# Two layers' front end on one core: layer 1's ada parts put between attention heads, one PSUM bank for probabilities, out product by row halves, router order

## What is computed

```python
hn = rmsnorm(x, g_mix); proj = hn @ w_in        # q, k, v, c_q, c_kv, k_pe, gate_a, gate_b
y_a = moba_attention(q_a, k_a, v_a)             # 8 heads, causal, 64 wide
y_b = causal_attention(q_b, k_b, v_b)           # 8 heads, 96 wide
merged = sigmoid(gate_a) * (y_a @ w_branch_a) + sigmoid(gate_b) * (y_b @ w_branch_b)
x = x + merged @ w_out
x = x + routed_experts(rmsnorm(x, g_ffn), ...)  # top 4 of 32 experts, clamped SwiGLU
hp = rmsnorm(x, g_ple); x = x + sigmoid(hp @ w_ple_gate) * (p @ w_ple_proj)
for l in range(2):
    shift, scale, gate = split(silu(c) @ w_ada[l] + b_ada[l], 3)
    ...
```

## Time and profile before

| what | value |
|---|---|
| median of 3 runs | 1425.66 us |
| the profiled execution | 1425.22 us, span 1423.0 us |
| PE busy | 1337.5 us (94%) |
| PEld, DVE, ACT, POOL busy | 712.5, 479.2, 316.1, 36.2 us |
| moved by DMA | 498.75 MB, mean 351 GB/s |
| chain that ended last | PE 60%, DMA 24%, DVE 6%, ACT 2% |

### The profile page before, as it was taken

The page is one execution under the profiler, slowest core; times in us unless marked ns, Lnnn a source line. Parts: engine busy times, 40 slices in busy tenths (PEclk is TensorE's granted clock), DMA queues, the critical chain, the costliest instruction groups (busy, mean ns, idle before and its releaser), DMA issues.

```text
span 1423.0 us, 16623 instructions
## 1 busy us (share of the span) xinstructions
PE 1337.5 (94%) x6794; PEld 712.5 (50%) x6794; DVE 479.2 (34%) x696; ACT 316.1 (22%) x416; POOL 36.2 (3%) x50
## 2 busy tenths in 40 slices
PE   8989999999999999999899999898999989999998
PEld 5758866334334333333333333333333336897996
DVE  3676665112112111211121111211112116775764
ACT  4254633011111110110111101111011114632531
POOL 2110100000000000000000000000000000000000
PEclk9999999999999999999999999999999999999999
DMA  9982397999999999999999999999999996355330
GB/s 326 387 323 89 107 380 322 418 428 428 428 428 428 428 429 428 429 428 427 429 429 428 428 429 428 427 429 429 428 429 429 428 408 207 120 183 192 125 120 30
DMA packets 76975, 498.75 MB, mean 351 GB/s; under 512 B 7095, under 2 KB 8586, under 8 KB 52362
## 3 DMA queue, kind: packets, MB, share of 16 engines
q1 hardware_dynamic: 75802, 496.06, 85.3%
q0 software_dynamic: 704, 2.10, 0.5%
q10 hardware_dynamic: 432, 0.07, 0.0%
HBM read 497.06 MB, written 1.05 MB: 350 GB/s over the span
## 4 chain that ended last, share of the span: by engine, by line
PE 60%; DMA 24%; DVE 6%; ACT 2%; issue 1%; POOL 0%; SPq 0%; DVEq 0%; ACTq 0%
PE ps L1765 31%; DMA ring<-in_w_gate_up_dram 21%; PE ps L1501 5%; PE ps L1503 5%; PE ps L1502 5%; PE ps L1759 3%; DMA arena<-in_w_gate_up_dram 2%; PE ps L1746 1%; PE ps L1830 1%; ACT arena L760 1%; PE ps L1522 1%; PE ps L1769 1%; PE ps L1523 1%; PE ps L1528 1%; DVE ring_low L891 1%
## 5 line engine op out<-in xcount | busy, mean ns | idle before, releaser
L1765 PE MATMUL ps<-ring,arena 128*64 128x512 f32 x2304 | 518.1, 600 | 33.1 <-DMA ring<-in_w_gate_up_dram 22.1
L1765 PEld LDWEIGHTS ps<-ring,arena 128*64 128x64 f32 x2304 | 159.4, 138 | 364.5 <-issue 300.3
L1765 PE MATMUL ps<-arena 128*64 128x512 f32 x768 | 175.2, 608 | 5.2 <-ACT arena L760 3.3
L1251 DVE TENSOR_SCALAR arena<-ps 128x512 f32<-128x512 f32 x32 | 22.1, 692 | 347.6 <-PE ps L1765 347.6
L753 ACT ACTIVATE arena<-arena 128x512 f32<-128x512 f32 x32 | 20.2, 630 | 498.6 <-DVE arena L1251 498.6
L1765 PEld LDWEIGHTS ps<-arena 128*64 128x64 f32 x768 | 53.7, 139 | 117.3 <-issue 102.2
L1503 PE MATMUL ps<-arena_highs,w_low 128*128 128x256 f32 x384 | 108.4, 282 | 0.0
L1210 DVE TENSOR_SCALAR esel<-const 128x128 fp32r<-128x128 f32 x49 | 12.6, 286 | 278.9 <-ACT arena L764 141.0
L764 ACT COPY arena<-ps 64x512 f32<-64x512 f32 x64 | 37.1, 580 | 239.6 <-PE ps L1765 239.2
L1230 DVE TENSOR_TENSOR X<-X,ps 128x1024 f32<-128x1024 f32 x34 | 41.4, 1218 | 124.2 <-PE ps L1759 124.2
L1501 PE MATMUL ps<-arena_highs,ring_highs 128*128 128x256 f32 x256 | 72.0, 281 | 2.3 <-DVE HT_r L1291 2.3
(11 more groups left out here) (284 smaller groups left out, 1591.9 us busy)
## 6 DMA issues: line engine op xcount, KB each, us to landing
ring<-in_w_gate_up_dram SPq DMA_DIRECT2D x96, 2048.0 KB, 31.2
ring<-in_w_down_dram SPq DMA_DIRECT2D x48, 2048.0 KB, 34.7
arena<-in_w_gate_up_dram SPq DMA_DIRECT2D x32, 2048.0 KB, 32.2
ring<-in_w_in_dram SPq DMA_DIRECT2D x38, 1024.0 KB, 7.2
arena<-in_w_down_dram SPq DMA_DIRECT2D x16, 2048.0 KB, 34.3
ring<-in_w_ada_dram SPq DMA_DIRECT2D x24, 1024.0 KB, 10.2
ring<-in_w_out_dram SPq DMA_DIRECT2D x12, 1024.0 KB, 7.4
ring<-in_w_ple_gate_dram SPq DMA_DIRECT2D x4, 1024.0 KB, 26.9
```

The lines of the kernel that those rows point to most:

```text
L1251: V.tensor_scalar(glu, ps[:, 0, :], LIMIT, None, ALU.min).then_inc(s["g_ready"], 1)
L1765: last = T.matmul(ps[at:at + CAP, bank, :], lhsT, w(g), start=False, stop=stop)
```

## The change

- Layer 1's twelve ada parts, with their chunks in `order1`, go into heads 0, 1, 2, 4, 5, 6, 8, 9, 10, 12, 13 and 14, each behind the head's `project`. They add into bank 3.
- The transposed probabilities of all heads go through bank 1; so a head's transposes wait for the copy of the head before, where they waited for the copy of two before. The pairs of kTb0, kTb1, mod0 and A0 change.
- ScalarE copies layer 1's ada rows out behind the cast of o0's first half, and TensorE waits for that ahead of A1 (`ada_out` 8). The rows go to the part of `const` that held the causal mask, and on to `tabs`. SyncE's `ada_moved(1)` stands behind the load of bin 4, ahead of bins 0 to 3.
- The out product goes over all (h, g) for row half 0, then over row half 1. The first columns of merged stand directly ahead of it, the second between.
- The router of half 1 comes ahead of both `choose`, its columns directly behind `route(0)`. Fillers: one ahead of `route(1)`, four between the counts, where two and three ada parts were.
- `yslot` is cleared by GpSimd, `shares(0)` goes to behind `routed`, and the gathered tokens are moved in two halves.

```diff
-        ada_rows = [view(24, 512), ht_flat[:, 1024:1536]]
-        ada_mods = [view(26, 512, "p (r n) -> p r n", r=4), ht_flat[:, 1536:2048].rearrange("p (r n) -> p r n", r=4)]
+        ada_rows = [view(24, 512), const[:, C_CAUSAL:C_CAUSAL + 512]]
+        ada_mods = [view(26, 512, "p (r n) -> p r n", r=4), tabs[:, 0:512].rearrange("p (r n) -> p r n", r=4)]
...
-        order1 += [(name, kh) for name in ("ga0", "ga1", "gb0", "gb1") for kh in range(2)]
-        order1 += [("A0", 0), ("B0", 0)] + [("ada1", i) for i in range(4)] + [("A1", 0), ("B1", 0)]
-        order1 += [("ada1", i) for i in range(4, 8)] + [(name, kh) for name in ("o0", "o1") for kh in range(2)]
-        order1 += [("ada1", i) for i in range(8, 2 * ADA_COLS)]
+        ada1_at = [h for h in range(2 * HEADS) if h % 4 != 3]
+        for j, (name, kh) in enumerate((name, kh) for name in ("ga0", "ga1", "gb0", "gb1") for kh in range(2)):
+            at_head = [[("ada1", ada1_at.index(h))] if h in ada1_at else [] for h in (2 * j, 2 * j + 1)]
+            order1 += at_head[0] + [(name, kh)] + at_head[1]
+        order1 += [("A0", 0), ("B0", 0), ("A1", 0), ("B1", 0)] + [(name, kh) for kh in range(2) for name in ("o0", "o1")]
...
-                  (("B1", 0), at64[:], None), (("o0", 0), at56[:], ("A0", 0)), (("o0", 1), ring11, ("B0", 0)),
-                  (("o1", 0), ring10, ("A1", 0)), (("o1", 1), at64[:], ("B1", 0))]
+                  (("B1", 0), at64[:], None), (("o0", 0), at56[:], ("A0", 0)), (("o1", 0), ring11, ("B0", 0)),
+                  (("o0", 1), ring10, ("A1", 0)), (("o1", 1), at64[:], ("B1", 0))]
...
-                             ("qTb0", 2, N), ("qTb1", 0, N), ("kTb0", 1, N), ("mod0", 0, N), ("kTb1", 2, N),
+                             ("qTb0", 2, N), ("qTb1", 0, N), ("kTb0", 2, N), ("kTb1", 0, N), ("mod0", 1, N),
                              ("gb0", 2, used1("gb0")), ("gb1", 2, used1("gb1")), ("yTa", 2, N), ("yTb", 0, N),
-                             ("A0", 1, used1("A0")), ("B0", 2, used1("B0")), ("A1", 0, used1("A1")),
+                             ("A0", 3, used1("A0")), ("B0", 2, used1("B0")), ("A1", 0, used1("A1")),
...
-        ADA_BANK = 7
+        ADA_BANK = [7, 3]
+        PROB_BANK = 1
...
-        RT_BANK, POS_BANK = 2 * U1["fT0"][0], 2 * U1["fT0"][0] + 1
+        RT_BANK, POS_BANK = [2 * U1["fT0"][0], 2 * U1["A0"][0]], 2 * U1["fT0"][0] + 1
...
             for k in (4, 0, 1, 2, 3):
                 phase1_left(k)
                 load(0, k)
+                if k == 4:
+                    ada_moved(1)
             sp.wait_ge(s["chunk_used1"], used1("o1"))
             load(0, GROUPS - 1)
             load(1, BINS - 1)
-            ada_moved(1)
...
+            pool.wait_ge(s["chunk_used1"], N1)
+            for a in yslot:
+                G.memset(a, 0.0).then_inc(s["y_cleared"], 1)
...
             w1_high("o0", 0)
+            ada_out(1)
+            w1_high("o1", 0)
             w1_high("o0", 1)
-            w1_high("o1", 0)
             w1_high("o1", 1)
...
+            for h in range(HALVES):
                 act.wait_ge(s["lg_ready"], h + 1)
                 A.activation(ex[:, h, :], lg[:, h, :], ACT.Exp, bias=st[:, 4 + h:5 + h]).then_inc(s["expd"], 1)
-            ada_out(1)
...
-                V.tensor_copy(probT[:, h % 2, :], ps[:, 2 * (h % 2) + 1, 0:3 * P]).then_inc(s["t_free"], 1)
+                V.tensor_copy(probT[:, h % 2, :], ps[:, PROB_BANK, 0:3 * P]).then_inc(s["t_free"], 1)
...
                 if g:
+                    w1_low("o1", 0)
                     w1_low("o0", 1)
-                    w1_low("o1", 0)
...
-            norm_of_x(0)
+            mean_of_x(0)
             columns_of_x(0)
+            power_of_x(0)
             low_part(0)
+            x_sum(1)
+            columns_of_x(1)
+            mean_of_x(1)
             choose(0)
-            shares(0)
-            x_sum(1)
-            norm_of_x(1)
-            columns_of_x(1)
+            power_of_x(1)
             choose(1)
...
-            run(V.memset(yslot[0], 0.0))
-            V.memset(yslot[1], 0.0).then_inc(s["y_ready"], 1)
-            shares(1)
+            for h in range(HALVES):
+                shares(h)
             join()
...
+            dve.wait_ge(s["y_cleared"], 2)
+            dve.sem_inc(s["y_ready"], 1)
             dve.wait_ge(s["routed"], 1)
-            dve.wait_ge(s["gather_done"], 1)
-            gathered()
+            for j, done in enumerate(("gather_half", "gather_done")):
+                dve.wait_ge(s[done], 1)
+                rows = slice(4 * j, 4 * j + 4)
+                ins = V.tensor_tensor(xg[:, rows, :], ps[:, 2 + j, :].rearrange("p (a b) -> p a b", a=4),
+                                      gain8[:, rows].unsqueeze(2).to_broadcast([P, 4, P]), ALU.mult)
+                if j:
+                    ins.then_inc(s["xg_ready"], 1)
+                else:
+                    run(ins)
...
             def transpose_probs(h):
-                bank = 2 * (h % 2) + 1
                 pe.wait_ge(s["prob_done"], h + 1)
-                if h >= 2:
-                    pe.wait_ge(s["t_free"], h - 1)
+                if h >= 1:
+                    pe.wait_ge(s["t_free"], h)
                 for b in range(3):
-                    last = T.transpose(ps[:, bank, b * P:b * P + P], prob[:, h % 2, b * P:b * P + P], ident)
+                    last = T.transpose(ps[:, PROB_BANK, b * P:b * P + P], prob[:, h % 2, b * P:b * P + P], ident)
                 last.then_inc(s["t_full"], 1)
...
+                    if h in ada1_at:
+                        ada_part(1, ada1_at.index(h))
...
-                if g:
-                    columns_of_merged(0)
-                ada_parts(1, 4 * g, 4 * g + 4)
-            columns_of_merged(1)
-
+                    if g + br == 1:
+                        pe.wait_ge(s["ada_out"], 8)
...
-            out_product(0, 0)
-            out_product(0, 1)
-            out_product(1, 0)
+            columns_of_merged(0)
+            for h in range(HALVES):
+                for g in range(2):
+                    out_product(h, g, (0,))
+            columns_of_merged(1)
+            for h, g in ((0, 0), (0, 1), (1, 0)):
+                out_product(h, g, (1,))
             columns_of_x(0)
-            out_product(1, 1, (0,))
+            out_product(1, 1, (1,))
             route(0)
-            out_product(1, 1, (1,))
-            ada_parts(1, 8, 10)
             columns_of_x(1)
+            keep_busy(2, 1)
+            route(1)
             pe.wait_ge(s["mask_done"], 1)
             count(0, before, 0)
             count(E, ones, 0)
             count(2 * E, ones, 0)
-            ada_part(1, 10)
-            route(1)
-            ada_part(1, 11)
-            keep_busy(2, 2)
+            keep_busy(2, 4)
...
+                if k == 3:
+                    last.then_inc(s["gather_half"], 1)
```

More of the change, by code:

```diff
@@ L241, in build @@
         out_stored dve_step pow_in pow_out tables_done
-        x_sums col_highs col_lows w1_highs w1_lows t1_highs mod1_full mod1_moved c_sigmoid cwide_zero cwide_ready q_ready k_ready mlaq_ready mlak_ready
+        x_sums y_cleared gather_half col_highs col_lows w1_highs w1_lows t1_highs mod1_full mod1_moved c_sigmoid cwide_zero cwide_ready q_ready k_ready mlaq_ready mlak_ready
         s_full s_free scored prob_done t_full t_free pv_done y_done
@@ L680, in ada_out @@
                 for r in range(0, P, 32):
-                    A.copy(ada_rows[l][r:r + ADA_COLS, :], ps[r:r + ADA_COLS, ADA_BANK, :]).then_inc(s["ada_out"], 1)
+                    A.copy(ada_rows[l][r:r + ADA_COLS, :], ps[r:r + ADA_COLS, ADA_BANK[l], :]).then_inc(s["ada_out"], 1)
             w1_high("ga1", 0)
@@ L1119, in columns_of_x, with mean_of_x, power_of_x @@
                               ).then_inc(moved1[p], 1)
-            def norm_of_x(h):
+            def mean_of_x(h):
                 dve.wait_ge(s["ffn_sums"], h + 1)
                 V.tensor_scalar(st[:, h:h + 1], st[:, h:h + 1], 1.0 / D, EPS, ALU.mult, ALU.add).then_inc(s["pow_in"], 1)
+            def power_of_x(h):
                 power()
@@ L1133, in choose @@
                 dve.wait_ge(s["rt_full"], h + 1)
-                run(V.scalar_tensor_tensor(lg[:, h, :], ps[:, RT_BANK, h * E:h * E + E], st[:, h:h + 1], b_rt,
+                run(V.scalar_tensor_tensor(lg[:, h, :], ps[:, RT_BANK[h], h * E:h * E + E], st[:, h:h + 1], b_rt,
                                            ALU.mult, ALU.add))
@@ L1537, in ada_part @@
                     at, n = 32 * k, 4 * (i % 2) + k
-                    last = T.matmul(ps[at:at + ADA_COLS, ADA_BANK, :],
+                    last = T.matmul(ps[at:at + ADA_COLS, ADA_BANK[l], :],
                                     cwide[:, n, ADA_COLS - 1 - i // 2:2 * ADA_COLS - 1 - i // 2],
@@ L1714, in route @@
                 for k in range(KC):
-                    last = T.matmul(ps[:, RT_BANK, h * E:h * E + E], HT[:, k, h * P:h * P + P], wr[:, k, :],
```

(1 more changed line is left out.)

1 line of the change is left out of this document (added).

## The result

| what | before | after |
|---|---|---|
| median | 1425.62 us (4 runs) | 1445.30 us (4 runs, 1442.46 to 1446.88) |
| profiled execution, span | 1425.22, 1423.0 | 1442.46, 1440.7 |
| first matmul of the expert loop | 246.95 | 269.50 |

The ratio is 1.0139 with a 95% interval of 1.0123 to 1.0155: **slower by 1.4%**, 19.7 us. The forecast was 1440.0, in a range of 1429 to 1446. The direction was right, and so was the mechanism (all bins are full, so the start of the expert loop sets the time); the delay was put too low. The measured time lies only 0.7 us under the top of the range, and its interval (1443.2 to 1447.7) reaches past it.

The account below looks back on a forecast made before the run. The stream of expert weights was taken as the bound, with the loop's start deciding past 249.9 us. Delays of 6.9 + 3.4 + 0.4 + 6.0 + 0.6 put it at 264.3, so 1425.66 + 14.4 = 1440.0, range 1429 to 1446.

Parts of the forecast that it names:

- The law: At the expert loop's start: with all eight bins full the stream stops, so a later start adds its delay one for one.
- point of decision: Loop start of 249.9 us (254.9 - 5.0): later starts make the kernel slower by just that, earlier ones faster.
- The gate chunks: Before the attentions: later places in the saturated DMA queue delay ScalarE's kv moves and TensorE's first scores by 6.9 us.
- Rival 1: Start of the attentions: gate chunks land as early as now, the 6.9 us goes, time 1431; chance 0.15.
- The first attention: Six ada parts 5.9, wait at head 4 used up -4.6, low clock +1.5, VectorE later +0.6: +3.4 us.
- The low clock behind the new wait: Ahead of head 0: a new wait of some 7.6 us brings the low clock, +1.5 us.
- the pairs and the second attention: Between attentions, kTb0 and kTb1 taking qTb0's and qTb1's pairs costs +0.4 us; second attention, with six parts, +6.0.
- The bank: One bank for transposed probabilities: last transposes of the second attention wait 0.1 us, all other heads 0.
- After the attentions: From the attentions to the loop: twelve ada parts leave, -11.8 us, new waits and fillers cost +12.4, sum +0.6.
- a gap like that of 3.10 before brings the low clock: +1.5: Ahead of the first out products: the wait of +3.3 us there lowers TensorE's clock, costing 1.5 us more.
- Rival 2: Room in the stream wins: gaps covered, loop starts at 243.6, before 249.9, time 1419 us; chance 0.10.
- Rival 3: Nothing measurable: the loop makes good TensorE's lateness, 1.9 us an expert faster than the stream, time 1426; chance 0.07.

Follow-up runs that it names:

- e3: Kernel before with ten pairs of filler matmuls in place of two ahead of the last count: 1426.89 us, ratio 1.0020.
- e5: Kernel before with three of layer 1's ada parts moved into TensorE's wait at head 4, summed in bank 3: 1419.41 us, ratio 0.9972.
- e10: e5's kernel with eight fillers in place of two ahead of the last counts: 1420.42 us, ratio 0.9972.
- e1: Changed kernel with layer 1's ada parts at heads 5 to 15, so the gate chunks come first in the queue again: 1439.21 us, ratio 1.0115.
- e4: Kernel before with all heads' transposed probabilities through PSUM bank 1 alone: 1424.42 us, ratio 1.0001.
- e6: Changed kernel with one filler in place of four ahead of the last counts: 1440.53 us, ratio 1.0125.
- e2: Changed kernel with SyncE's sixteen issues storing layer 1's ada rows put back behind the last bins' loads: 1445.98 us, ratio 1.0162.
- e7: Changed kernel with merged's first columns cast ahead of o1's second half, and half 1's sum ahead of half 0's low part: 1443.15 us, ratio 1.0141.
- e8: Changed kernel with the edits of e1, e6 and e7 together: 1434.91 us, ratio 1.0080.
- e9: Kernel before without the two fillers ahead of the last counts: 1423.57 us, ratio 0.9999.

## Why the prediction was right, and where it fell short

**The law held, its point was 1 to 2 us off.** The point of decision, a loop start of 249.9, was worked out from 5.0 us for use, issue and start of a transfer. By the spans of the late kernels it is 1423.0 - 1171.1 = 251.9. Of these 2.0 us, 1.1 belong to the point: measured at the stream's end it is 246.95 + 887.3 - 883.3 = 251.0, from which the 2.1 us of e3's span follow. The other 0.9 lies in the last 32 matmuls, which the clock made longer in the kernel before; why is open. Later is one for one, as said. But the sentence that a loop that starts earlier makes the kernel faster is refuted: beside e5, the 5.6 us by which e10's loop starts later cost 0.3 us of span (1.0 at the stream's end, where e10 is just past the crossing), and beside the kernel before, with the same loop start, the earlier bins are what is left to make e10 faster. e5's gain is that its bins are issued 6.0 us earlier.

**The gate chunks: +6.9 forecast, 6.1 measured against the kernel before** (87.44, 81.31) and 6.35 against e1. Landing by number in a saturated queue gave 84.2 for ga0's second half; its cast begins at 83.38. Rival 1 falls. The rule named beside it (the Trainium skill, DMA: Bandwidth & Descriptors, "Queues, rings and completion order") allows another order of completion; no run here showed one between whole chunks.

**The first attention: +3.4 forecast, 5.1 measured.** Its end moved from 125.10 to 136.32, 11.2 us, of which 6.1 are the scores'. The parts did use up most of the wait at head 4 (0.86 left of 3.10), and the clock behind it was 1.00, where it was 0.57:

```profile
112.00:116.00 4.00, 3.71 (x20) 2.29 (x20) 3.90 (x9) 1.19 (x5) 1.70 (x1) 1.00 1.05 390
```

The low clock behind the new wait of 7.46 came as forecast (0.50 from 87 to 90). But one part costs 1.1 us among heads (pitch of a head with one 5.55, 4.45 without), not 0.98. With the pairs and the second attention, also at 1.1 each, the columns of y come 18.7 later where 16.7 were forecast. The bank was rightly put at next to nothing (e4).

**After the attentions: +0.6 forecast, +3.8 measured** (84.8 us for 81.0), the largest miss. The waits were sized well: 1.69 ahead of A1 (1.9), 3.62 ahead of the out products (3.3), 2.48 at their second half (2.6; the trace names nothing that ended it), 1.93 ahead of the second x columns (2.0). What was too small is the term "a gap like that of 3.10 before brings the low clock: +1.5". In the profiled execution the clock stayed at 1.00 behind the wait of 3.62, and such a stretch came behind the 2.48 (0.75 from 230 to 235, seven matmuls at 0.63 us where 0.39 to 0.47 is usual). A second one, which the forecast didn't have, lies among the columns of x, the router and the fillers: 1.88 for columns that take 1.03, 1.92 for two filler records that take 1.0, 5.38 for eight that take 3.6 (half of the sixteen that took 7.13 in e10). It costs another 3.6 us. The terms as measured are -11.8 + 1.7 + 3.6 + 1.4 (the seven matmuls) + 2.5 - 1.7 + 1.9 + 2.7 (fillers at the high clock) + 3.6 = 3.9. The note "VectorE needs less for both choices than the four fillers last" was right, and so the fillers stood bare (e6).

**The sum.** At the loop's start 269.50 against 264.3, +5.2, less 1.1 for the point and 0.9 for the last expert: 3.3 us of span too little (1440.7, forecast 1423.0 + 14.4). That these two went the other way is luck: with 2.0 us more the time would have been above the range. The rest of the 5.3 us on the median is that the profiled execution of after was the fastest of its four.

**The other rivals.** Rival 2, room in the stream, is true of the transfers and worthless: bin 0 is issued 8.1 us earlier and all bins are in before the loop, so the second limit holds. With three parts in place of twelve the same idea won (e5). Rival 3 falls by the result itself, and by e3, where the loop did not make good the 2.1 us beyond the crossing.

## What to carry to other kernels

Before work is moved out of the way of a prefetched stream, find which of two limits holds: when the stream's first loads are issued, or when the consumer starts with all buffers full. Only the later one pays, and a change can cross from one to the other, as this did. Independent work is worth most where an engine waits: three parts in a 3.1 us wait gained 3.9 us, while twelve spread evenly took the cover from four hand-overs behind the attentions and put a needed transfer three places back in a full queue. The gain of 3.9 us came through the loads, which could be issued earlier because TensorE was done earlier with what lay in their bins.

## What the hardware showed beyond that

- The same wait doesn't always bring the low clock. The out products behind a wait of 3.62 us ran at 1.00 in the changed kernel and in e6, and partly at the low level in e1 and e2 (0.67 from 210 to 215 in e1); behind 3.17 us at 1.00 in e7, low in e8 (0.66). That moves the loop's start by 1.3 to 2.7 us between kernels that do the same there, and perhaps between executions of one, of which only one each has a trace.
- The clock differed by kernel in the last expert too, some 900 us behind the loop's start: its last 32 matmuls took 7.09 us in the changed kernel, e1, e6, e7, e8 and e10, 8.0 to 8.1 in the kernel before, e3, e4, e5 and e9, and 8.78 in e2. Why is open.
- The clock also falls with hardly a wait: in e7, without the wait of 1.93, it was at 0.50 from 255 to 260, behind transposes and 32-column products with gaps under 1 us. What is won ahead of such a stretch can be given back in it: the eight filler records took 6.48 us there and 5.38 in the changed kernel.
